# Two transformer blocks on one core: the shift columns of two early units summed on VectorE, and two weight splits ahead of the root

## What is computed

```python
def rms_norm(x, g):
    return x * rsqrt(mean(x * x, axis=-1) + EPS) * g
def modulate(h, shift, scale):
    return h * (1 + scale) + shift
...
sh1, sc1, gt1, sh2, sc2, gt2, sh3, sc3, gt3 = split(silu(c) @ w_ada + b_ada, 9)
h = modulate(rms_norm(x, g_ffn1), sh1, sc1)
x = x + 0.5 * gt1 * swiglu(h, w1_gu, w1_down)
h = modulate(rms_norm(x, g_mix), sh2, sc2)
proj = h @ w_in                      # q, k, v and five gates
...
x = x + gt2 * (merged @ w_out)
h = modulate(rms_norm(x, g_ffn2), sh3, sc3)
x = x + 0.5 * gt3 * swiglu(h, w2_gu, w2_down)
```

## Time and profile before

| | |
|---|---|
| median of 3 runs | 2146.86 us (2146.65 to 2148.67) |
| profiled execution | 2147.49 us, span 2145.7 us |
| TensorE busy | 2109.5 us, 98% of the span |
| VectorE, ScalarE, GpSimd busy | 1231.0, 861.9, 114.0 us |
| granted TensorE clock, mean | 0.992 |
| weight loads of 512 KB by SyncE | 389, median 3.6 us from issue to landing |

### The profile page before, as it was taken

One profiled execution on the slowest core, in us unless ns is written; L12 is line 12 of the kernel. 1 busy time (PEld: TensorE's weight loads), 2 busy tenths in 40 slices (PEclk: granted clock), 3 DMA queues, 4 the chain that ended last, 5 costly groups with the idle time before them and its releaser, 6 DMA issues. The chain is left out here.

```text
span 2145.7 us, 27246 instructions
## 1 busy us (share of the span) xinstructions
PE 2109.5 (98%) x10112; PEld 1712.7 (80%) x10112; DVE 1231.0 (57%) x1992; ACT 861.9 (40%) x1331; POOL 114.0 (5%) x117
## 2 busy tenths in 40 slices
PE   8999999999999999999999999999999999999998
PEld 7988888877777778878888887777777778888886
DVE  6887776766666445453333347778665454343444
ACT  6522222252343442342222236665775344232233
POOL 2000000022000000010000012000002010000001
PEclk8999999999999999999999999999999999999999
DMA  8655454534222323323333323122223213333332
GB/s 326 213 196 177 157 176 157 184 111 120 88 75 74 95 92 119 97 69 99 97 98 98 98 83 105 60 61 78 80 68 118 69 59 90 104 93 96 98 98 69
DMA packets 66777, 238.41 MB, mean 111 GB/s; under 512 B 7848, under 2 KB 10024, under 8 KB 65904
## 3 DMA queue, kind: packets, MB, share of 16 engines
q1 hardware_dynamic: 60768, 218.81, 31.7%
q0 software_dynamic: 3728, 16.08, 2.4%
q10 hardware_dynamic: 2176, 2.10, 0.3%
HBM read 230.12 MB, written 4.21 MB: 109 GB/s over the span
## 5 line engine op out<-in xcount | busy, mean ns | idle before, releaser
L1245 DVE TENSOR_TENSOR wlo<-raw,whi 128x1024 fp32r<-128x1024 f32 (+1 forms) x352 | 427.8, 1215 | 264.0 <-ACT whi L611 261.0
L2116 PE MATMUL bank<-hhi,whi 128*128 128x512 f32 (+1 forms) x1408 | 546.0, 388 | 5.5 <-DVE hlo L1254 4.1
L611 ACT ACTIVATE whi<-raw 128x1024 fp32r<-128x1024 f32 (+1 forms) x352 | 367.2, 1043 | 437.2 <-PE bank L2118 388.6
L2118 PE MATMUL bank<-hhi,wlo 128*128 128x512 f32 (+1 forms) x1408 | 539.1, 383 | 0.0
L2117 PE MATMUL bank<-hlo,whi 128*128 128x512 f32 (+1 forms) x1408 | 538.8, 383 | 0.0
L2116 PE MATMUL bank<-ghi,whi 128*128 128x512 f32 x1016 | 398.9, 393 | 2.8 <-DVE wlo L1245 2.8
L2118 PE MATMUL bank<-ghi,wlo 128*128 128x512 f32 x1016 | 395.6, 389 | 0.0
L2117 PE MATMUL bank<-glo,whi 128*128 128x512 f32 x1016 | 395.3, 389 | 0.0
L2116 PEld LDWEIGHTS bank<-hhi,whi 128*128 128x128 f32 x1408 | 267.6, 190 | 58.7 <-DVE wlo L1245 6.9
L2118 PEld LDWEIGHTS bank<-hhi,wlo 128*128 128x128 f32 x1408 | 267.6, 190 | 51.2
L2117 PEld LDWEIGHTS bank<-hlo,whi 128*128 128x128 f32 x1408 | 267.7, 190 | 50.0 <-issue 0.7
(11 more groups left out here) (315 smaller groups left out, 1980.6 us busy)
## 6 DMA issues: line engine op xcount, KB each, us to landing
raw<-w SPq DMA_DIRECT2D x389, 512.0 KB, 3.6
work<-w SPq DMA_DIRECT2D x12, 512.0 KB, 10.8
raw<-w SPq DMA_DIRECT2D x16, 384.0 KB, 3.1
gated_in<-gated_in POOLq DMA_DIRECT2D x40, 64.0 KB, 1.9
gated_in<-w SPq DMA_DIRECT2D x4, 512.0 KB, 9.6
xT<-x_t POOLq DMA_DIRECT2D x1, 2048.0 KB, 12.0
kv_hbm<-work POOLq DMA_DIRECT2D x2, 1024.0 KB, 4.8
work<-w POOLq DMA_DIRECT2D x4, 512.0 KB, 5.3
```

What stands on the lines that cost most here:

```text
L611: nc.scalar.activation(whi[v % 2][:, 0:kc * P], raw[u % 4][:, 0:kc * P], ACT.Copy).then_inc(w_hi, 1)
L1245: nc.vector.tensor_tensor(wlo[v % 2][:, 0:kc * P], raw[u % 4][:, 0:kc * P], whi[v % 2][:, 0:kc * P].bitcast(F32), ALU.subtract).then_inc(w ...
L2116: nc.tensor.matmul(dst, wh[:, ws], hi[:, c, :], start=c == 0, stop=False)
L2118: ins = nc.tensor.matmul(dst, wl[:, ws], hi[:, c, :], start=False, stop=c == kc - 1)
```

## The change

- `shift_fold` is new on VectorE. For each of the two un-normalised units it multiplies the raw weights with the shift (one value per partition and chunk, broadcast over 128 columns) into half of `gated_in` (`shift_tile`), and adds the halves three times: 1024, 512, 256, 128 columns are left. It stands behind the residuals of chunk 5 and of chunk 6.
- TensorE then needs one matmul per unit with a column of ones (L2177 in the new numbering), in place of eight with the shift.
- SyncE's wait for `shift_done` is gone.
- Units v+2 and v+3 get buffers of their own, `ahead`, which lie over `merged` and `prob`. So ScalarE's and VectorE's splits of them wait for no other unit, and stand ahead of `stats` on ScalarE and ahead of the first scaling on VectorE.
- VectorE copies the shift columns before it waits for the root; the two `early_take` products move among the scalings.

```diff
+        shift_tile = [gated_in[:, 2 * i * S:2 * (i + 1) * S] for i in range(2)]
...
+        ahead = [nc.alloc_sbuf_tensor_at(f"ahead{i}", [P, DC * P], F32R, offset=work_at + 4 * (at[0] + i * DC * P))
+                 for i in range(4)]
...
+        AHEAD = (V_MIX + 2, V_MIX + 3, V_FFN[1] + 2, V_FFN[1] + 3)
+        def split_buffers(v):
+            return (ahead[2 * (v % 2)], ahead[2 * (v % 2) + 1]) if v in AHEAD else (whi[v % 2], wlo[v % 2])
...
-                if shifts is not None:
-                    sp.wait_ge(shift_done, shifts)
...
-                if v >= 2 or not isinstance(dv, int):
+                if not isinstance(dv, int) or v >= 2 and v + 4 * dv not in AHEAD:
                     act.wait_ge(unit_done, v - 1 + 4 * dv)
...
+            def shift_fold(n, k):
+                e, u, w = EARLY[n], raw_of((V_MIX, V_FFN[1])[EARLY[n]] + k), shift_tile[k]
+                step = 4 * (2 * e + k)
+                dve.wait_ge(landed[u % 4], 16 * (u // 4 + 1))
+                s = mods[:, SH[n] * DC:(SH[n] + 1) * DC].unsqueeze(2).to_broadcast([P, DC, P])
+                nc.vector.tensor_tensor(w.rearrange("p (a b) -> p a b", b=P), raw[u % 4][:].rearrange("p (a b) -> p a b", b=P),
+                                        s, ALU.mult).then_inc(shift_step, 1)
+                for fold in range(3):
+                    half = D >> (fold + 1)
+                    dve.wait_ge(shift_step, step + fold + 1)
+                    nc.vector.tensor_tensor(w[:, 0:half], w[:, 0:half], w[:, half:2 * half], ALU.add).then_inc(shift_step, 1)
...
                         residual(v + c, c, mod(2 if f == 0 else 8, c))
+                        if f == 0 and part == 2 and c in (DC - 3, DC - 2):
+                            shift_fold(N_MIX, c - DC + 3)
...
                 residual(V_WO + c, c, mod(5, c))
+                if c in (DC - 3, DC - 2):
+                    shift_fold(N_FFN2, c - DC + 3)
...
-                pe.wait_ge(mods_done, (8, 11)[EARLY[n]])
+                pe.wait_ge(shift_step, 8 * (EARLY[n] + 1))
                 for k in range(2):
-                    u = raw_of(v + k)
-                    pe.wait_ge(landed[u % 4], 16 * (u // 4 + 1))
-                    for c in range(DC):
-                        ins = nc.tensor.matmul(bank[6][:, k:k + 1], raw[u % 4][:, c * P:(c + 1) * P], shift(n, c),
-                                               start=c == 0, stop=c == DC - 1)
-                    ins.then_inc(shift_done, 1)
+                    ins = nc.tensor.matmul(bank[6][:, k:k + 1], shift_tile[k][:, 0:P], ones[:, 0:1], start=True, stop=True)
+                ins.then_inc(shift_done, 1)
```

More of the change, by code:

```diff
@@ L205, in build @@
         conv_out = place(S)
+        place(-(at[0] % -8))
+        ahead = [nc.alloc_sbuf_tensor_at(f"ahead{i}", [P, DC * P], F32R, offset=work_at + 4 * (at[0] + i * DC * P))
+                 for i in range(4)]
         merged = place(DC, S)
@@ L507, in _ @@
             down2 = V_FFN[1] + 60
-            run(V_MIX, V_FFN[1], row0, shifts=2)
-            run(V_FFN[1], down2, row0 + V_FFN[1] - V_MIX, shifts=4)
+            run(V_MIX, V_FFN[1], row0)
+            run(V_FFN[1], down2, row0 + V_FFN[1] - V_MIX)
             run(down2, V_GATE, DC, FF_PARTS[2])
@@ L661, in early_norm @@
                 split(v + 1)
+                split(v + 2)
+                split(v + 3)
+                nxt[0] = v + 4
                 stats(n)
-                shifted_hi(n, 0)
-                shifted_hi(n, 1)
+                for c in range(3):
+                    shifted_hi(n, c)
                 early_take(n, v, *takes[0])
-                split(v + 2)
-                for c in range(2, 5):
+                for c in range(3, 7):
                     shifted_hi(n, c)
@@ L670, in early_norm @@
                     early_take(n, v + 1, *takes[1])
-                split(v + 3)
-                nxt[0] = v + 4
-                for c in range(5, DC):
-                    shifted_hi(n, c)
+                shifted_hi(n, DC - 1)
             def early_take(n, v, t, func):
@@ L1262, in early_norm @@
             def early_norm(n, v, takes):
+                split(v + 2)
+                split(v + 3)
+                nxt[0] = v + 4
+                dve.wait_ge(shift_done, EARLY[n] + 1)
+                nc.vector.tensor_copy(shift_col[:, EARLY[n], :], bank[6][:, 0:2]).then_inc(shift_in, 1)
                 dve.wait_ge(rstd_done, n + 1)
@@ L1267, in early_norm @@
                 shifted_lo(n, 0)
-                dve.wait_ge(shift_done, 2 * EARLY[n] + 2)
-                nc.vector.tensor_copy(shift_col[:, EARLY[n], :], bank[6][:, 0:2]).then_inc(shift_in, 1)
-                early_take(n, v, takes[0])
                 norm_scale(n, 2)
                 shifted_lo(n, 1)
-                split(v + 2)
-                norm_scale(n, 3)
-                shifted_lo(n, 2)
-                norm_scale(n, 4)
+                early_take(n, v, takes[0])
+                for c in range(3, 7):
+                    norm_scale(n, c)
+                    shifted_lo(n, c - 1)
                 early_take(n, v + 1, takes[1])
-                shifted_lo(n, 3)
+                norm_scale(n, 7)
+                shifted_lo(n, 6)
                 if n == N_FFN2:
@@ L1283, in early_norm @@
                         ALU.mult).then_inc(evac[(v + 1) % 2], 1)
-                split(v + 3)
-                nxt[0] = v + 4
-                for c in range(5, DC):
-                    norm_scale(n, c)
-                    shifted_lo(n, c - 1)
-                shifted_lo(n, DC - 1)
+                shifted_lo(n, DC - 1)
+            def shift_fold(n, k):
[9 more added lines that the diff above has]
+                    nc.vector.tensor_tensor(w[:, 0:half], w[:, 0:half], w[:, half:2 * half], ALU.add).then_inc(shift_step, 1)
             def early_take(n, v, t):
```

17 lines of the change are left out of this document (11 added, 6 removed).

## The result

The changed kernel takes 2152.8 us (median of 15 runs); the kernel before takes 2147.2 us in the runs beside it. The ratio is 1.0026, with a 95% interval of 1.0019 to 1.0033: slower by a quarter of a per cent, where 2138.5 us was forecast. One of its 15 runs took 7177.9 us and is left out of the ratio; without it the median is 2152.6. The profiled execution took 2154.08 us with a span of 2152.3 us (before: 2147.49 and 2145.7).

The account below looks back on a forecast made before the run. TensorE, busy 98%, was taken as the bound. Gains of 1.75 us (first seam) and 6.7 us (second), in all 8.4, took the profiled 2147.49 to 2139.1 us, median 2138.5; range 2135.8 to 2142.2 for 8 in 10.

Parts of the forecast that it names:

- part 4: From the root on, both seams: shorter chain, TensorE's pair stalling on remainders; gains 1.75 us at the first, 6.7 at the second.
- part 2: Four sums on VectorE: 2.65 us each, nothing added for GpSimd; 1.5 us of new stall at the first seam, none at the second.
- A matmul's cost: TensorE's normal stream: 0.227 us for each record of 512 columns.
- Passes: TensorE, both seams: four records of 0.44 us together replace 32; saves 3.05 and 3.5 us, 2.5 more if the clock stays up.
- Stalls on the splits at the first seam: TensorE waits for VectorE's splits, late behind the sums: 0.4 and 0.9 us, plus 0.1 each for a restart.
- Residual of chunk 7: VectorE at the first seam: chunk 7 is added at 460.4 instead of 458.64, 1.75 us later.
- Root: ScalarE's root of the norm comes 3.7 us later at the first seam and 1.9 us later at the second.
- Chain from the root: VectorE's first scaling to last remainder: 12.7 us at the first seam instead of 18.2, about 14 at the second.
- SyncE's wait: Loads of the fifth unit and on go out some 6 us earlier; no wait for them on the path either side.
- Rival C: Both seams: root later, chain behind it keeps its length; 5.6 us later in sum, 2152.5 us; chance 0.06.
- Rival D: Sums cost x us more beside GpSimd: 2x at first seam, 2(x - 0.7) at second; 2143 at x = 1.5; chance 0.06.
- Rival A: Second seam's clock fall is chance, absent in the runs that set the median; gain 5.5 us, 2141.4; chance 0.16.

Follow-up runs that it names:

- e1: The changed kernel with both early_take products moved forward on VectorE and ScalarE, behind the remainders of chunks 0 and 2; 2143.75 us, 0.9979 of before.
- e9: The changed kernel with GpSimd's additions of the squares of chunks 5 and 6 cut to one column ahead of both seams; 2150.39 us, 1.0014 of before.
- e5: As e1, but each sum cut up: products behind the residuals of chunks 4 and 5, additions behind those of 6 and 7; 2140.12 us, 0.9966 of before.
- e8: The kernel before with the 32 one-column passes replaced by two matmuls, and no sums (shift columns not computed); 2140.48 us, 0.9968 of before.
- e4: The changed kernel with the 32 one-column passes and SyncE's wait back, and no sums; 2147.37 us, 0.9990 of before.
- e10: As e4, but with the early_take products moved forward as in e1; 2142.08 us, 0.9972 of before.
- e6: As e5, with ScalarE's three splits ahead of the square of chunk 7, own buffers for units v+1 and v+2, VectorE's constants earlier; 2133.26 us, 0.9932 of before.
- e7: As e1 with the four sums left out, four one-column copies in place of each; 2139.08 us, 0.9966 of before.

## Why the prediction was wrong

**The step that failed is in part 4**: "The pair then stalls on remainders of chunks 2, 3 and 5 to 7", and its like at the second seam. The pair's two units write the banks of the two un-normalised units, so they begin only when `early_take` has emptied these. The text counts both products in the chain and prices them, and even says that "the products no longer wait for TensorE"; it doesn't turn the sentence round. In the kernel before, VectorE waited for TensorE there, 1.35 us at the first seam and 4.54 at the second:

```profile
945.90 0.69 DVE L1294 TENSOR_TENSOR gated_in<-bank,rstd 128x512 f32<-128x512 f32 x1 [4.54 <-PE bank L2171]
```

Once the root is later and TensorE earlier, TensorE waits for VectorE. The order of the change puts the second product behind the remainder of chunk 5 and the scaling of 6, and this, not the seventh remainder, lets the second unit begin. By e1 it is worth 4.3 + 4.9 = 9.2 us. 4.0 of these are the clock, which the text held to be safe ("A fall in the new kernel is less likely"): it fell at both seams, behind the stalls that the text didn't have.

**The second failed step is in part 2**: "VectorE's own rows do not grow there, so I add nothing". The row on which it stood, shows the case in which GpSimd comes second: VectorE's operation at 456.85 had begun before GpSimd's at 456.98, and GpSimd's row is the long one (1.77 us; 1.28 at 45.60, where it runs alone; 1.44 at 452.75, where it starts 0.46 us behind VectorE's operation). Where GpSimd comes first it is VectorE's operation that waits. The trace of before had that too, early in the span, which I did not look up (VectorE's halvings of another tile, and GpSimd; at 1285.41 and later there are remainders of 1.78 us as well):

```profile
35.88 2.13 DVE L1476 TENSOR_TENSOR work<-work 128x512 f32<-128x512 f32 x2 [0.51 <-ACT work L759]
```

```profile
36.44 2.70 POOL L546 TENSOR_TENSOR square_sum<-square_sum,square 128x512 f32<-128x512 f32 x2 [2.99 <-ACT square L627]
```

The same two halvings take 1.15 us elsewhere: 0.98 us more, just what a sum was to cost more than the 2.65 us of the forecast. The Trainium skill has the rule, in "SBUF — State Buffer", sections "SBUF: two separate sides" and "Who interferes with whom": a VectorE instruction with two inputs in SBUF and a GpSimd instruction that reads SBUF exclude each other, and whichever starts first keeps the shared pair for its whole instruction. The rows here agree, e9 and e5 above all; and where VectorE came first, GpSimd's addition ends 1.15 us behind VectorE's end (458.75 behind 457.60, 454.19 behind 453.04), whatever its own row shows.

With these two the ledger closes to some tenths, if they simply add up; no run repairs both and leaves all else. At the first seam the forecast was -1.75 us against before and the profile shows +4.59, 6.3 apart: 4.3 for the banks (e1) and 1.9 for the hold (e9's root, and its idle time in that crossing). At the second it was -6.7 and the profile shows +0.34, 7.0 apart: 4.9 for the banks, 1.27 for the hold and the 1.18 us of `bank[0]` that e1 still has, 7.35 together. e5, which has early takes and moves the hold to another place, comes near the forecast: its crossings are 2.3 and 5.8 us shorter than before, where 1.75 and 6.7 were forecast.

Point by point, the rest:

- *A matmul's cost*: 0.227 us is right, but not by the division shown (5.00 / 23 is 0.217): it is the spacing of starts, 4.08 us for 18 matmuls.
- *Passes*: the next matmul starts 0.36 us behind the 4 records (468.42 to 468.78), forecast 0.44. Their worth of 9.05 us of TensorE's own time was 7.6 us of the whole (e8).
- *Stalls on the splits at the first seam*: forecast 0.4 and 0.9, measured 1.25 and 1.70, and 0.28 and 0.73 once the hold is gone.
- *Residual of chunk 7*: forecast 1.75 later; 9.95 - 8.16 = 1.79 in e9, 3.7 in the changed kernel.
- *Root*: forecast 3.7 and 1.9 later; by VectorE's first scaling 3.85 and 1.90 in e9, 5.8 and 3.2 in the changed kernel.
- *Chain from the root*: forecast 12.7 and about 14; 474.14 to 486.90 is 12.8, and at the second seam 949.32 to 963.3 is 14.0. This was the term I had least hold on, and it came out to a tenth.
- *SyncE's wait*: nothing on either side, as said.
- *Rival C* has the time (2152.5) but not the mechanism: its chain keeps its 18.2 us, and the real one got shorter by 5.4. That its time came out is luck.
- *Rival D* has the right mechanism and the right first term (x = 0.97, 2x = 1.94 us). Its second, 2(x - 0.7) = 0.54, measured 1.27, has the wrong slack. 0.7 us is what the split had left before TensorE wants it; VectorE's own list from one residual to the next had less, 0.25 us in e9, where no sum is held. In the changed kernel the residuals follow each other 6.08 and 6.07 us apart instead of 5.44, 0.63 late for each sum.
- *Rival A*: it remains open whether the fall at the second seam of before is in most of its runs. In the profiles of before, e4 and e10 the clock fell in or behind the passes at five seams of six, so it was no accident of one row. But one profile is taken of each kernel, and without the passes it fell at 10 seams of 18, there behind stalls. The runs do differ: of the 20 of the kernel before beside e9 and e10, the five with a mean granted clock of 0.995 or 0.996 took 2143.3 to 2145.5 us, and 14 of the other 15 took 2146.1 to 2151.7.

The text's own last sentence named all of it as what would make it wrong: a clock that still falls at either seam, a sum of over 3.5 us, and a pair whose end hangs on something other than the remainders.

## What to carry to other kernels

For every buffer that a moved engine will want, ask who empties it, and where the one that empties it stands in its own list after the change; a wait that the profile shows in one direction turns round when the other side becomes the late one. A price read beside a concurrent operation holds only for that order of starts: look for a row with the other order as well. Small work put into an engine's list in front of something that another engine waits for should be cut into pieces that fit each gap (e5). What feeds a serial chain should not be delayed to shorten what stands behind it: e6, which among other things avoids that, is the fastest here.

## What the runs showed of the hardware

- A 256-column addition on VectorE goes from 424 to 1392 ns, and a 512-column operation from 0.75 to 1.8 us, when it reads two operands from SBUF and starts while an addition of GpSimd (1.28 us alone) runs. Rows of VectorE with one of their inputs in PSUM do not grow beside it (`xT<-bank` at 1287.11 in the kernel before, 0.74 us, inside GpSimd's row of 1286.60 to 1288.35).
- The granted clock can fall to 0.50 while TensorE is recorded busy without a gap, behind 32 one-column passes (3.5 to 3.8 us): five seams of six in the profiles that have them. The Trainium skill, "TensorE: Matmul & The Clock Gate", section "HAM oscillation — how this bites in real kernels", lays falls to idle gaps; the falls of the changed kernel (behind stalls of 2.4 to 3.3 us) agree with it in kind, those behind the passes don't.
- The length of a stall does not tell by itself whether the clock falls. With the same stalls of 1.0 and 1.8 us behind the un-normalised units of the second seam, e5 kept a clock of 1.00 and e7 fell to 0.50 behind them; e8 fell at its first seam behind stalls of 1.02 and 1.40 us and kept 1.00 at its second behind 1.33, 1.02 and 0.83. What decides that is not shown by any run here.
